# A 12-stage fp32 transformer kernel on one core: scan squares, dt rows, first banded logits and norms reordered, MLA values in 384 columns, the last product finished tile by tile

## What is computed

```python
def rmsnorm_2(x, g):
    xf = x.astype(jnp.float32)
    var = jnp.mean(xf * xf, axis=-1, keepdims=True)
    return (xf * lax.rsqrt(var + EPS)).astype(x.dtype) * g
...
# first block, per layer: x += 0.5*swiglu(rmsnorm(x)); u = rmsnorm(x) @ w_in -> mLSTM branch (hA), banded
# attention branch (window 128, 8 query and 2 key heads of 64, q and k normed), two sigmoid gates; x += mixed @ w_out;
# x += 0.5*swiglu(rmsnorm(x)); x += sigmoid(rmsnorm(x) @ w_ple_gate) * (p @ w_ple)
...
# second block, per layer
        h = rmsnorm_2(x, norm_mix_g[l])
        uv, z, xbc, dt_raw, c_q, c_kv, k_rope = split_cols(h @ w_in[l])
        y_a = gmlp_mixer(...)
        y_b = ssd_mixer(...)      # dt = softplus(dt_raw + dt_bias); a_h = cumsum(dt_h * A); 6 heads of 64, chunks of 128
        y_c = mla_mixer(...)      # kv = (rmsnorm_2(c_kv) @ w_kvb): 6 heads x (64 keys + 64 values), c_q 384 wide, c_kv 256
        x = x + jnp.concatenate([y_a, y_b, y_c], axis=-1) @ w_out[l]
        x = x + squared_relu_mlp(rmsnorm_2(x, norm_mlp_g[l]), mlp_w1[l], mlp_w2[l])
    return rmsnorm_2(x, final_norm_g)
```

## Time and profile before

| | us |
|---|---|
| median of three runs | 3418.3 (3418.28 to 3418.5) |
| the profiled execution, whole | 3419.56 |
| its span, first to last instruction | 3417.8 |
| PE busy in it | 3387.1 (99%) |
| DVE, ACT, POOL busy | 1630.9, 1046.1, 1544.5 |

### The profile page before, as it was taken

The page is one execution under the profiler, slowest core; times in us unless marked ns, Lnnn a source line. Parts: engine busy times, 40 slices in busy tenths (PEclk is TensorE's granted clock), DMA queues, the critical chain, the costliest instruction groups (busy, mean ns, idle before and its releaser), DMA issues.

```text
span 3417.8 us, 43447 instructions
## 1 busy us (share of the span) xinstructions
PE 3387.1 (99%) x15470; PEld 2740.0 (80%) x15470; DVE 1630.9 (48%) x1988; ACT 1046.1 (31%) x1393; POOL 1544.5 (45%) x1160
## 2 busy tenths in 40 slices
PE   8999999999999999999999999999999999999998
PEld 7888876788888888887678888887888887788887
DVE  5442235754423544223565442376580727657161
ACT  3222234332223322223433222236421124632112
POOL 4444442354444544443335444443354544335452
PEclk9999999999999999999999999999999999999999
DMA  4333422233333333333223333332233333223332
GB/s 150 98 92 98 111 75 68 74 99 98 98 99 93 99 98 98 95 109 80 62 74 100 97 98 101 93 94 54 68 98 98 94 99 81 49 74 105 94 97 80
DMA packets 496158, 311.26 MB, mean 91 GB/s; under 512 B 41792, under 2 KB 454827, under 8 KB 496043
## 3 DMA queue, kind: packets, MB, share of 16 engines
q1 hardware_dynamic: 494316, 307.21, 30.9%
q10 hardware_dynamic: 1727, 2.45, 0.2%
HBM read 305.94 MB, written 3.67 MB: 91 GB/s over the span
## 4 chain that ended last, share of the span: by engine, by line
issue 38%; PE 30%; POOL 26%; DVE 3%; DVEq 1%; POOLq 0%; ACT 0%; DMA 0%; ACTq 0%
POOL wl L495 26%; PE bank L533 4%; PE bank L514 4%; PE bank L519 4%; PE bank L518 4%; PE bank L537 4%; PE bank L539 4%; PE bank L1149 1%; PE mb L1176 1%; PE bank L540 1%; PE mb L593 0%; DVEq L1723 0%; DVE xl L1724 0%; PE mb L1087 0%; DVE xa_l L1733 0%
## 5 line engine op out<-in xcount | busy, mean ns | idle before, releaser
L495 POOL TENSOR_TENSOR wl<-raw,wh 128x512 fp32r<-128x512 f32 x1152 | 1543.4, 1361 | 1836.3 <-ACT wh L1299 1836.1
L1299 ACT ACTIVATE wh<-raw 128x1024 fp32r<-128x1024 f32 x576 | 608.5, 1057 | 1655.4 <-PE bank L514 862.5
L533 PE MATMUL bank<-xh,wh 128*128 128x512 f32 x2384 | 935.0, 392 | 1.5 <-DVE tmp_all L1708 1.5
L537 PE MATMUL bank<-xl,wh 128*128 128x512 f32 x2384 | 929.1, 390 | 0.0
L539 PE MATMUL bank<-xh,wl 128*128 128x512 f32 x2086 | 813.3, 390 | 0.0
L533 PEld LDWEIGHTS bank<-xh,wh 128*128 128x128 f32 x2384 | 448.5, 188 | 108.6 <-issue 13.3
L537 PEld LDWEIGHTS bank<-xl,wh 128*128 128x128 f32 x2384 | 448.5, 188 | 92.6 <-issue 0.5
L514 PE MATMUL bank<-hh,wh 128*128 128x512 f32 (+1 forms) x1216 | 473.2, 389 | 0.0
L519 PE MATMUL bank<-hh,wl 128*128 128x512 f32 (+1 forms) x1216 | 473.0, 389 | 0.0
L518 PE MATMUL bank<-hl,wh 128*128 128x512 f32 (+1 forms) x1216 | 473.0, 389 | 0.0
L539 PEld LDWEIGHTS bank<-xh,wl 128*128 128x128 f32 x2086 | 392.4, 188 | 82.4
(11 more groups left out here) (404 smaller groups left out, 3156.0 us busy)
## 6 DMA issues: line engine op xcount, KB each, us to landing
raw<-in_ffn_wi_dram SPq DMA_DIRECT2D x176, 512.0 KB, 3.7
raw<-in_mlp_w_dram SPq DMA_DIRECT2D x128, 512.0 KB, 3.7
raw<-in_w_in_dram SPq DMA_DIRECT2D x102, 512.0 KB, 3.7
raw<-in_ffn_wo_dram SPq DMA_DIRECT2D x88, 512.0 KB, 3.6
raw<-in_w_out_dram SPq DMA_DIRECT2D x32, 512.0 KB, 3.8
raw<-in_w_ple_gate_dram SPq DMA_DIRECT2D x16, 512.0 KB, 3.8
raw<-in_w_a_dram SPq DMA_DIRECT2D x8, 512.0 KB, 3.3
raw<-in_w_b_dram SPq DMA_DIRECT2D x8, 512.0 KB, 3.3
```

Source lines behind the costliest of these rows:

```text
L495: last = gp.tensor_tensor(wl[j][:, part], raw[j % RAW_SLOTS][:, part], wh[j][:, part].bitcast(F32), ALU.subtract)
L533: first = pe.matmul(out[0:width, :], h[:, c:c + width], rh[:, k, :], start=k == 0, stop=False)
L537: pe.matmul(out[0:width, :], h[:, c:c + width], rl[:, k, :], start=False, stop=False)
L1299: act.activation(wh[n % SPLIT_SLOTS][:], raw[n % RAW_SLOTS][:], ACT.Copy).then_inc(s.hi_ready, 1)
```

## The change

Eight edits; each engine's list is rewritten where it needs it.

- First norm of the program: DVE no longer splits the sum of squares, and PE multiplies it by ones in one unrounded matmul. The other norms keep the split. All ten `norm`s on ACT get a one-element Sqrt ahead of two slabs.
- swa: logits(0) ahead of the second half of gate unit 9; DVE makes hal in two parts ahead of gate tile 8, and gate tile 9 behind the first masked logits.
- dt rows: DVE makes -|x| (one 6x512 operation), ACT's Abs goes, and slabs U_C to U_C + 3 are rounded later, behind copies and weights of the scan.
- Scan's squares: DVE adds the five c_sq tiles to two, PE multiplies two instead of five, one unit later, into B6. The ACT square stands one step earlier. DVE reads unit U_Z + 2 between heads 4 and 5.
- Values: a slab is one half of the contraction with six heads, so 12 matmuls of 384 columns take the place of 24 of 192.
- norm_behind: all xh/xl pairs stand ahead of the reciprocal.
- End: q = 4 to 7 run tile by tile; tile 3 in halves of 256 tokens, the second into bank B6, with token_sums(0) inside. Turns, inverses, roots, scalings and stores go token block by token block.

```diff
--- before.py
+++ after.py
@@ (SP) the value weights: two slabs, one for each half of the contraction, with all six heads @@
-                for u, (h0, heads, c0) in enumerate(((0, 6, 0), (0, 3, 64), (3, 3, 64))):
+                parts = (((0, 0, 6, 0), (1, 0, 6, 0)), ((0, 0, 3, 64), (0, 3, 6, 64)), ((1, 0, 3, 64), (1, 3, 6, 64)))
...
@@ (SP) stores @@
-                sp.wait_ge(s.fin_copied, t + 2)
+                sp.wait_ge(s.fin_copied, t + 1)
...
@@ (PE) new helper @@
+            def token_sums(part):
+                for t in range(2 * part, 2 * part + 2):
+                    pe.matmul(mb[:, 3, t:t + 1], acc[:, t * P:(t + 1) * P], ones[:, 0:1], start=True, stop=False)
+                    last = pe.matmul(mb[:, 3, t:t + 1], tmp[3][:, t * P:(t + 1) * P], ones[:, 0:1], start=False, stop=True)
+                last.then_inc(s.ss_psum, 1)
@@ (PE) def sum_squares @@
+                if whole:
+                    pe.matmul(B4, ones[:], acc[:], start=True, stop=True).then_inc(s.ss_psum, 1)
+                    return
@@ (PE) def first_units: sum_squares(B, L, k) becomes sum_squares(B, L, k, setup) @@
@@ (PE) swa @@
-                gate_unit(L, 9, 1)
                 pe.wait_ge(s.kk_copied, at(L, 1, 1))
-                pe.wait_ge(s.qk_bc_read, at(L, 5, 5))
+                pe.wait_ge(s.qk_bc_read, at(L, 5, 4))
...
                 logits(0)
+                gate_unit(L, 9, 1)
+                pe.wait_ge(s.qk_bc_read, at(L, 5, 5))
@@ (PE) ssd @@
                     elif i == 1:
-                        pe.wait_ge(s.c_squared, at(L, 1, 1))
-                        for k in range(3):
-                            pe.matmul(B7[0:64, :], ones[:, 0:64], c_sq[:, k, :], start=k == 0, stop=k == 2)
-                        for k in range(2):
-                            last = pe.matmul(B7[64:P, :], ones[:, 0:64], c_sq[:, 3 + k, :], start=k == 0, stop=k == 1)
-                        last.then_inc(s.c_ss, 1)
                         more_in2(L, U_Z + 1)
                         decays(4)
                         decays(5)
-                        pe.wait_ge(s.c_read, at(L, 1, 1))
+                        pe.wait_ge(s.y_added, at(L, 3, 1))
+                        pe.wait_ge(s.c_ready, at(L, 2, 2))
+                        pe.matmul(B6[0:64, :], ones[:, 0:64], c_sq[:, 0, :], start=True, stop=True)
+                        pe.matmul(B6[64:P, :], ones[:, 0:64], c_sq[:, 3, :], start=True, stop=True).then_inc(s.c_ss, 1)
@@ (PE) mla.values @@
-                        out = bank[(B.base_tile + T2_KVB + 3 + t) % TILE_BANKS][:, part * 192:part * 192 + 192]
-                        for k in range(2):
...
+                        out = bank[(B.base_tile + T2_KVB + 3 + t) % TILE_BANKS][:, 0:384]
+                        tok = slice(t * P, (t + 1) * P)
+                        last = three(out, ckh[:, part, tok], ckl[:, part, tok], h[:, 0:384], l[:, 0:384], part == 0, part == 1,
+                                     new=t == 0)
@@ (PE) the last half of the last down product @@
+                            for d in range(3):
+                                for q in range(4, 8):
+                                    if d == 0:
+                                        take_slab(B, L, n1 + q)
+                                    last = part(d, q)
+                                last.then_inc(s.tile_ready, 1)
+                            for q in range(4, 8):
+                                last = part(3, q, tok=TOK_A)
+                            last.then_inc(s.tile_ready, 1)
+                            for q in range(4, 7):
+                                part(3, q, last_b, TOK_B, q == 4)
...
+                            token_sums(0)
+                            part(3, 7, last_b, TOK_B).then_inc(s.tile_ready, 1)
@@ (PE) the end: turns by token tile, token_sums(1) after the first tile @@
@@ (ACT) norm @@
+                act.activation(small[:, 61:62], ones[:, 0:1], ACT.Sqrt)
@@ (ACT) swa @@
-                act.wait_ge(s.ml_bc_read, at(L, ML_H, ML_H))
-                act.activation(hah[:], num_sb[:], ACT.Copy).then_inc(s.ha_rounded, 1)
+                for pair in range(2):
+                    act.wait_ge(s.ml_bc_read, at(L, ML_H, 2 * pair + 2))
...
@@ (ACT) ssd @@
-                ahead(Block2, L, S2_IN + U_C, 1)
                 act.wait_ge(s.dt_pre, at(L, 1, 1))
-                act.activation(tmp[1][0:SSD_H, :], tmp[3][0:SSD_H, :], ACT.Exp, scale=-1.0)
+                act.activation(tmp[1][0:SSD_H, :], tmp[3][0:SSD_H, :], ACT.Exp)
...
@@ (DVE) norm_behind @@
-                for j in range(2):
+                for j in range(4):
                     x_times_gain(j, g)
                 inverse_mean(B, L, k)
-                for j in range(2, 4):
-                    x_times_gain(j, g)
@@ (DVE) swa: hal in two halves ahead of gate_tile(L, 8); gate_tile(L, 9) behind biased(0) @@
@@ (DVE) gmlp @@
+                dve.scalar_tensor_tensor(out=tmp[3][0:SSD_H, :], in0=tmp[2][0:SSD_H, :], scalar=-1.0, in1=tmp[2][0:SSD_H, :],
+                                         op0=ALU.mult, op1=ALU.min).then_inc(s.dt_pre, 1)
@@ (DVE) ssd, i == 0, ahead of y_add(0) @@
+                        dve.tensor_tensor(c_sq[:, 0, :], c_sq[:, 0, :], c_sq[:, 1, :], ALU.add)
+                        dve.tensor_tensor(c_sq[:, 3, :], c_sq[:, 3, :], c_sq[:, 4, :], ALU.add)
+                        dve.drain()
+                        dve.tensor_tensor(c_sq[:, 0, :], c_sq[:, 0, :], c_sq[:, 2, :], ALU.add).then_inc(s.c_ready, 1)
@@ (DVE) ssd, i == 2 @@
+                        if h == SSD_H - 1:
+                            more_in2(L, U_Z + 2)
@@ (DVE) the end @@
+            def token_inverse(part):
+                dve.wait_ge(s.ss_psum, norm_no(Last, None, 0) + part)
+                invert(small[:, 2 * part:2 * part + 2], mb[:, 3, 2 * part:2 * part + 2], 1.0).then_inc(s.inv_var, 1)
```

More of the change, by code:

```diff
@@ L1552, in ssd @@
                 last.then_inc(s.xs_copied, 1)
-                ahead(Block2, L, S2_IN + U_C + 1, 1)
                 def weights(h):
@@ L1734, in early_x, with sum_half @@
                                          op0=ALU.mult, op1=ALU.subtract).then_inc(s.xa_ready, 1)
-            def sum_half(B, L, k, half):
+            def sum_half(B, L, k, half, whole=False):
                 dve.wait_ge(s.sq_ready, half_no(B, L, k, half))
@@ L1743, in sum_half @@
                     dve.drain()
-                    dve.scalar_tensor_tensor(out=acc[:], in0=acc[:], scalar=EPS / P, in1=var[:], op0=ALU.add, op1=ALU.add)
-                    dve.drain()
-                    last = split(sum_h[:], sum_l[:], acc[:])
+                    last = dve.scalar_tensor_tensor(out=acc[:], in0=acc[:], scalar=EPS / P, in1=var[:], op0=ALU.add, op1=ALU.add)
+                    if not whole:
+                        dve.drain()
+                        last = split(sum_h[:], sum_l[:], acc[:])
                 last.then_inc(s.ss_ready, 1)
@@ L1760, in inverse_mean, with norm @@
                 dve.reciprocal(var[:], B4).then_inc(s.inv_var, 1)
-            def norm(B, L, k, g, made=4, ahead_of_sum=KT):
+            def norm(B, L, k, g, made=4, ahead_of_sum=KT, whole=False):
                 dve.drain().then_inc(s.x_final, 1)
@@ L1814, in ffn @@
             def ffn(L, k, g, g_next, t, silu0):
-                norm(Block1, L, k, g, made=5 if L and k == 0 else 4)
+                norm(Block1, L, k, g, made=5 if L and k == 0 else 4, whole=L == 0 and k == 0)
                 if L == 0 and k == 0:
@@ L1958, in swa @@
                     dve.tensor_tensor(num_sb[:, h, :], num_sb[:, h, :], mb[:, h, :], ALU.mult).then_inc(s.ml_bc_read, 1)
+                for pair in range(2):
+                    heads = slice(2 * pair, 2 * pair + 2)
+                    dve.wait_ge(s.ha_rounded, at(L, 2, pair + 1))
+                    last = dve.tensor_tensor(hal[:, heads, :], num_sb[:, heads, :], hah[:, heads, :].bitcast(F32), ALU.subtract)
+                last.then_inc(s.ha_ready, 1)
                 gate_tile(L, 8)
@@ L2389, in _ @@
                             split(hh[:, j, :], hl[:, j, :], tb[:]).then_inc(s.hidden_ready, 1)
-                    for j in range(KT):
+                    for j in range(KT - 1 if L and half else KT):
+                        if L and half and j > 5:
+                            more_squares(4)
+                            more_squares(5)
                         add_x(B, L, t0 + HALF2 + j, j, inc=2 if half and j == KT - 1 else 1)
```

175 lines of the change are left out of this document (101 added, 74 removed).

## The result

The changed kernel takes 3399.54 us in the median of five runs (3397.93 to 3402.54) against 3418.5 (3418.28 to 3420.58): a ratio of 0.9948, 95% interval 0.9938 to 0.9959. It is 19 us faster; 26.3 were forecast, and 3399.5 lies above the range of 3387.5 to 3398.5. Its profiled execution took 3401.84, its span is 3400.1, 17.7 less than before.

What follows compares the result with a forecast made beforehand. PE, busy 99% of the span, was taken as the bound, so only its waits, instructions and low clock give time. Terms of 20.95 us, 26.3 with the clock, off 3418.3 gave 3392.0; 3387.5 to 3398.5 holds 8 in 10.

Steps and rivals of the forecast that it cites:

- First norm: Program's first norm: without DVE's conversions PE no longer waits for sum_l, 1.7 us; full clock behind it, 1.4 more.
- Banded attention: Attention in two layers: earlier hal and logits remove PE's waits of 0.9 and 1.05 with restarts, 2.3 a layer, 4.6 us.
- dt rows: dt rows ahead of the scan: shorter ACT chain removes PE's waits for scan and rows_hl, 2.2 + 2.5 = 4.7 us.
- what is late next: Behind the dt rows: the later-rounded slabs named as tightest place, first ready about 2319.7 against 2321.5 on PE, slack 1.8.
- Scan's squares: Scan: two c_sq matmuls instead of five gain 1.76 us a layer; DVE's additions, about 2.1, hidden by 24 matmuls.
- Last products: Scan's last products: DVE done 1.8 us earlier, four instead of eight products behind unit U_Z + 2's tile; gain 0.5 a layer.
- Values: Values in two layers: 48 matmuls of 384 columns at 0.174 us replace 96 of 192, 10.7 - 8.35 = 2.35 us.
- MLP norms: MLP norms: earlier table load against two xh/xl pairs ahead of the reciprocal; between +1.9 and -1.5 us, taken as 0.
- End: Program's end: first store 3.5 us earlier, last 1.75, DMA queues only partly the bound; gain 3.1, between 2.3 and 3.6.
- Clock: PE's three half-clock stretches, behind first norm and both layers' dt rows, stay at full clock once waits go; 5.4 us.
- or moves to another place: Rival: PE's clock stays low in the dt rows or elsewhere; 4.0 to 5.4 us less, 3396 to 3397.5; chance 0.18.
- A new wait in the scan: Rival: additions delay y_add(0), or slab U_C comes late; 1 to 2 us a layer, 3394 to 3396; chance 0.13.

Runs made afterwards that it cites:

- e7: The kernel of e9 with the first norm as before the change (sum split, two rounded matmuls): 3397.58 us.
- e12: The kernel before the change with two of its edits alone, the first norm and the dt rows: 3410.80 us.
- e2: The changed kernel with ACT's rounding of one scan slab moved behind the last silu, so that POOL splits it later: 3395.75 us.
- e1: The changed kernel with the scan's squares as before: five unrounded matmuls, no additions on DVE: 3399.17 us.
- e11: The kernel of e9 with the gating (y times silu z) in two parts, two thirds ahead of y_add(2): 3392.52 us.
- e14: The kernel of e8 with the values as before the change, 96 matmuls of 192 columns instead of 48 of 384: 3396.09 us.
- e8: The changed kernel with one scan slab rounded behind the silu and three instead of four xh/xl pairs ahead of the MLP norms' reciprocal: 3393.75 us.
- e10: The kernel of e9 with the end as before the change, in all its engines' lists: 3397.08 us.
- e3: The changed kernel with DVE's two rotary sums moved behind the products of heads 4 and 5: 3399.89 us.
- e4: The changed kernel with the orders of e2 and e3, and three xh/xl pairs instead of four ahead of the MLP norms' reciprocal: 3394.38 us.
- e9: The kernel of e8 with DVE's rotary sums moved behind y's gating, the scan's last product: 3394.18 us.
- e13: The kernel of e8 with the gating in two parts as in e11, rotary sums still ahead of head 4's products: 3394.14 us.

## Why the prediction was wrong, point by point

- **First norm, 1.7 + 1.4.** Gave 3.56 in the trace and 3.4 by e7, so it was 0.3 to 0.5 short: the wait with its restart is worth 2.1 (2.6 with the later wait of e7), the clock 1.4 in the trace before (3.56 less 2.1), and e7's three slower executions lie 0.7 to 1.4 above its fastest.
- **Banded attention, 4.6.** Gave 4.1 by the marks, 2.15 in each attention alone. The waits for lg are gone from the list; the mechanism held, and 0.25 of the first layer's gain is lost at 1106 us.
- **dt rows, 4.7 + 4.0 of clock.** Gave 8.65 in the two stages themselves, right to 0.1. But the part's question "what is late next" was answered with the slab that PE might lack right behind; what the roundings moved was POOL's split some 50 us on, under the scan's last products. e12 shows it: 1.0 us more waiting a layer on the kernel before, from the dt rows' edit (the first norm's lies 2300 us away).
- **Scan's squares, 3.5.** Gave 2.45 on PE. The five matmuls' 2.72 a layer became 0.91 for two, as forecast, but 0.4 went to a pause between the two rows_hl products (0.74 apart instead of 0.33, with a wait of 0.24 for sd_w). The step that failed is the next sentence: the three additions, "about 2.1 us", were said to be hidden by unit U_Z + 1's 24 matmuls. They cost 3.0 (the third ran beside POOL), and I compared them only with y_add(0), the next thing waited for, and not with DVE's own chain up to head 5.
- **Last products, +1.0.** Gave -5.75. This is the term that was wrong, in sign. I let DVE be done 1.8 us earlier by the new order, on the clock of the trace before, with quartets of 1.9. Counted from the scan's first products, DVE was through with the third pair's sd_p at 23.8 us before and at 24.6 after, 0.8 later and not 1.8 earlier, while PE asked for them 1.25 earlier. DVE's chain from the additions on had no gap in which a delay could be taken up, and head 5's quartet took 4.01 under POOL's split. Beside the 2.1 counted for the additions there were 0.95 more for them, 0.4 for heads 2 and 3 and 2.1 for head 5: 3.4 of delay by POOL. Without it DVE would have been through at about 2354.2, 1.0 ahead of PE (an estimate from these rows). e2 takes away head 5's part and 4 us of waiting go; e1 takes away the additions and the same 4 us go: either alone is enough. Behind the 2.6 us wait the clock fell in the first layer, another 1.7. The gain of 0.5 a layer that the new order was to bring doesn't show without POOL either: from the second pair's products to y_sq e2 needs 19.57 where the kernel before needs 19.29, and only e11 (18.62) gets there. The place of unit U_Z + 2's tile between heads 4 and 5 was not undone by itself.
- **Values, 2.35.** Right, by trace (2.36) and e14. No row had that width and 0.174 was a choice between two estimates (three quarters of 0.227 is 0.170, not 0.171), so the third digit is luck.
- **MLP norms, 0.** +0.62 and -0.67. The bounds held; what decides is whether the fourth xh starts a fraction of a microsecond ahead of POOL or behind it. With three pairs ahead (e8) the wait is gone in both layers, though the third pair is through only 0.04 before POOL.
- **End, 3.1.** 3.05 in the trace, 2.9 by e10. The last three stores land 1.2 us apart, as all four did before, so the queue still bounds the end of the tail.
- **Clock, 5.4.** All three falls are gone, and e12's profiled execution shows the same on the kernel before. That one new fall came in its place was the rival "or moves to another place".
- **The rivals.** "A new wait in the scan" was the case that came, at 0.13, and priced at 1 to 2 us a layer; at the last products the two layers came out 4.2 and 2.5 us short of their forecast. The additions were named, but with y_add(0) as what they delay; what came late was head 5. And the size was missed: I added up the operations of one engine at their undisturbed durations, though the earlier trace rows held two that were stretched beside POOL, and I had used that contention in the norms and left it out in the scan.

The Trainium skill (SBUF — State Buffer, Who interferes with whom) says that a vector instruction with two SBUF inputs contends with a GpSimd instruction that reads SBUF, that the shared port pair is an exclusive lock, and that the order of issue decides who blocks. The sd_p products have two such inputs, POOL's split reads SBUF, and the traces agree: the quartets take 1.94 and 4.01, and e2's 1.93; head 5's second product, begun at 2354.30, 0.03 behind POOL's subtraction, takes 1.67 where e2's takes 0.61, while that subtraction keeps its 1.28.

## What to carry to other kernels

When a change lets one engine run ahead, redo the sum for the next stage with the other engines' whole chain, not with the one operation that is waited for. If a vector engine's chain there has no idle row, an operation added to it is paid as soon as the small margin at the chain's end is used up (1.0 us here), whatever lies beside it on the matrix engine. And moving an engine's work moves what it releases: a rounding that comes 0.3 us earlier relative to the products put POOL's split under their end and cost 1.0 us of waiting a layer (e12); placed behind a later step (e2) it left the wait at the 1.1 us of the kernel before.

## What the runs showed of the hardware

The clock fell to half behind waits of 1.8 and 3.1 us in e3, and behind 2.6 us in the changed kernel's first layer; behind the same 2.6 in its second layer, and behind 2.1 in e7's profiled execution, it stayed full. So behind a wait of some 2 us the fall is a matter of chance here. Four executions of a kernel without such waits lie within 0.2 to 0.9 us (e1, e4, e8, e9, e11, e13, e14), where the kernel before spreads over 7. The 384-column rounded matmul starts 0.174 us behind the one before it, the 256-column one 0.12 and the 192-column one 0.111, so from 256 to 192 columns next to nothing is saved. A quartet of masked products takes DVE 1.93 us alone and 4.01 beside two of POOL's subtractions.
